# Segment decays of a Mamba-2 scan in a hybrid decoder layer: from products of TensorE to running sums spread by DMA

## What is computed

```python
a_cum = jnp.cumsum(adt, axis=-1)
decay = jnp.exp(segsum(adt))                 # exp(cs[l] - cs[s]) for s <= l, else 0
cb = jnp.einsum("bclhn,bcshn->bhcls", cc, bc)
y_diag = jnp.einsum("bhcls,bcshp->bclhp", cb * decay, xc)
to_end = jnp.exp(a_cum[..., -1:] - a_cum)
states = jnp.einsum("bclhn,bclhp->bchpn", bc * to_end[..., None], xc)
# scan over chunks: h -> chunk_decay * h + states, from h0 = 0
y_off = jnp.einsum("bclhn,bchpn->bclhp", cc * from_start[..., None], prev)
y = (y_diag + y_off) + d_skip * x            # then gate with SiLU(z), RMSNorm in 2 groups
```

## Time and profile before

| | before |
|---|---|
| median of 3 runs | 1161.25 us (1160.11 to 1161.86) |
| profiled execution, its own time | 1160.93 us |
| its span | 1159.0 us |
| TensorE busy | 1096.3 us, 95% |
| VectorE busy | 872.1 us, 75% |
| ScalarE busy | 548.6 us, 47% |
| GpSimd busy | 242.4 us, 21% |
| mean granted clock of TensorE | 0.975 |

### The profile page before, as it was taken

One profiled execution on the slowest core, in us unless ns is written; L12 is line 12 of the kernel. 1 busy time (PEld: TensorE's weight loads), 2 busy tenths in 40 slices (PEclk: granted clock), 3 DMA queues, 4 the chain that ended last, 5 costly groups with the idle time before them and its releaser, 6 DMA issues.

```text
span 1159.0 us, 14934 instructions
## 1 busy us (share of the span) xinstructions
PE 1096.3 (95%) x5144; PEld 876.8 (76%) x5144; DVE 872.1 (75%) x1137; ACT 548.6 (47%) x964; POOL 242.4 (21%) x235
## 2 busy tenths in 40 slices
PE   2699999999999999969999999999999999999997
PEld 2578767666777777747888888888888888888885
DVE  5769577767559566587888888888888886776687
ACT  3631255555553343565454444454445455454453
POOL 2100011121212333124333333333333100000012
PEclk7699999999999999989999999999999999999999
DMA  9988311001132101104344343434353496733224
GB/s 342 328 252 300 111 37 37 19 20 37 37 110 91 55 37 55 55 37 146 119 153 139 133 152 119 158 129 158 109 170 109 143 370 220 237 100 98 93 91 164
DMA packets 115359, 152.71 MB, mean 132 GB/s; under 512 B 15148, under 2 KB 75117, under 8 KB 115309
## 3 DMA queue, kind: packets, MB, share of 16 engines
q1 hardware_dynamic: 114989, 151.00, 38.9%
q0 software_dynamic: 320, 1.06, 0.3%
HBM read 121.10 MB, written 30.95 MB: 131 GB/s over the span
## 4 chain that ended last, share of the span: by engine, by line
PE 85%; DVE 6%; ACT 3%; DMA 2%; issue 1%; POOL 1%; SPq 1%; DVEq 0%; POOLq 0%; ACTq 0%
PE ps L2283 34%; PE ps L1938 24%; PE ps L2348 17%; PE ps L1977 2%; PE ps L2003 1%; PE ps L1991 1%; PE ps L2127 1%; DVE big L1255 1%; DMA raw<-in_w_in_dram 1%; ACT big L973 1%; DMA scratch<-in_rel_bias_dram 1%; PE ps L2219 1%; PE ps L2042 1%; DVE a_lo L1524 0%; DVE scratch L1462 0%
## 5 line engine op out<-in xcount | busy, mean ns | idle before, releaser
L1938 PE MATMUL ps<-a_hi,w_hi 128*128 128x512 f32 x416 | 146.1, 429 | 9.0 <-DVE a_lo L1315 6.2
L1938 PE MATMUL ps<-a_lo,w_hi 128*128 128x512 f32 x416 | 132.3, 396 | 0.0
L1938 PE MATMUL ps<-a_hi,w_lo 128*128 128x512 f32 x416 | 131.6, 395 | 0.0
L2348 PE MATMUL ps<-w_hi,a_hi 128*128 128x512 f32 x308 | 119.9, 389 | 0.2 <-DVE a_lo L1771 0.2
L2348 PE MATMUL ps<-w_hi,a_lo 128*128 128x512 f32 x308 | 119.8, 389 | 0.0
L2348 PE MATMUL ps<-w_lo,a_hi 128*128 128x512 f32 x308 | 119.8, 389 | 0.0
L1938 PEld LDWEIGHTS ps<-a_hi,w_hi 128*128 128x128 f32 x416 | 73.6, 192 | 32.6 <-issue 21.9
L1167 ACT ACTIVATE w_hi<-raw 128x512 fp32r<-128x512 f32 x77 | 48.8, 634 | 98.2 <-PE ps L2348 88.4
L1087 ACT ACTIVATE scratch<-ps 128x512 f32<-128x512 f32 x88 | 52.3, 595 | 88.8 <-PE ps L2283 88.7
L1938 PEld LDWEIGHTS ps<-a_hi,w_lo 128*128 128x128 f32 x416 | 78.9, 190 | 18.3
L1938 PEld LDWEIGHTS ps<-a_lo,w_hi 128*128 128x128 f32 x416 | 78.9, 190 | 18.2 <-issue 0.5
(11 more groups left out here) (246 smaller groups left out, 2431.5 us busy)
## 6 DMA issues: line engine op xcount, KB each, us to landing
big<-in_w_ada_dram SPq DMA_DIRECT2D x24, 1024.0 KB, 9.0
raw<-in_w_up_dram SPq DMA_DIRECT2D x22, 512.0 KB, 5.0
big<-in_w_up_dram SPq DMA_DIRECT2D x22, 512.0 KB, 4.6
big<-in_w_down_dram SPq DMA_DIRECT2D x22, 512.0 KB, 6.4
down_weight_sums<-big SPq DMA_DIRECT2D x22, 512.0 KB, 3.4
raw<-down_weight_sums SPq DMA_DIRECT2D x44, 256.0 KB, 2.8
ffn_hidden<-big SPq DMA_DIRECT2D x21, 512.0 KB, 2.6
big<-ffn_hidden SPq DMA_DIRECT2D x21, 512.0 KB, 7.9
```

What stands on the lines that cost most here:

```text
L1938: mm = pe.matmul(out, lhs_of[a], rhs_of(b, j), start=first and p == 0, stop=last and p == 2)
L2348: mm = pe.matmul(bk, a[:, ts], rhs_op(s)[w], start=fresh and m == 0, stop=last and m == 2, skip_group_check=s // KH in (J6, J3, J7))
```

## The change

The decays exp(cs[l] - cs[s]) are no longer made from sums on TensorE for each chunk.
- `dt_sum` makes one more product, the running sums of all chunks with heads on partitions (`sum_rows`, 64 rows of 128), and VectorE also takes the negated sums as columns (`neg_sums`). SP stores the rows to DRAM (`rows_d`) and, for each chunk, `load_decay(i)` reads the chunk's 4 KB row into all 128 partitions of `decay`, once y_diag of the chunk before has read it.
- GpSimd adds a mask of -1e30 where s > l (`decay_mask`, in place of `decay_terms`). ScalarE makes eight exponentials of 128x128 a chunk, each with a column of `neg_sums` as bias.
- `ssd_weights` multiplies by the CB products straight from bank 7. `cbm` and its product by `upper` are gone, with the two products against `strict`.
- Chunk 0 has no y_off and no decay of the state, since the state is zero; the last chunk makes no B rows, no state product and no state. GpSimd's memset of the state is gone.
- The lists are put in another order: on TensorE state_product(i) stands right behind y_diag(i), z_transpose(0) goes into the last input unit, and projection 0 ahead of y_off(1). On VectorE the attention half of the low parts goes from behind mixed_norm to ahead of ssm_rows of the block before. On ScalarE the attention half of the high parts and the exponentials of chunk i+1 go ahead of gated_squares(i).
- The semaphores of the token sums (t1 to t4) are merged into one.

The core of the diff:

```diff
+            def load_decay(i):
+
+                if i >= 1:
+                    sp.wait_ge(s_yd, i)
+                sp.dma_start(scratch[:, 2048:3072], rows_d[i:i + 1, :].to_broadcast([P, H * P])).then_inc(s_kl, 16)
...
+                if k == 0:
+                    sp.wait_ge(s_kr, 1)
+                    sp.dma_start(rows_d.rearrange("b (h l) -> (b h) l", h=H), sum_rows).then_inc(s_ks, 16)
+                    sp.wait_ge(s_ks, 16)
+                    load_decay(0)
...
+                if k == 6:
+                    load_decay(1)
             sp.wait_ge(s_wlo, U_OUT + 4)
             load_xr(0)
             load_xr(1)
+            load_decay(2)
...
             for b in range(NB):
+                if b + 3 < NB:
+                    load_decay(b + 3)
                 sp.wait_ge(s_mx, b + 1)
...
-            def decay_terms(i):
-
-                if i >= 1:
-                    pool.wait_ge(s_yd, i)
+            def decay_mask(i):
+
+                pool.wait_ge(s_kl, 16 * (i + 1))
                 for g in range(GROUPS):
-                    adt = dtv[:, ADT, i * H + 4 * g:i * H + 4 * g + 4].unsqueeze(2).to_broadcast([P, 4, P])
-                    tri = upper.unsqueeze(1).to_broadcast([P, 4, P])
-                    pool.tensor_tensor(decay[:, g, :].rearrange("p (h l) -> p h l", h=4), tri, adt,
-                                       ALU.mult).then_inc(s_rd, 1)
+                    dg = decay[:, g, :].rearrange("p (h l) -> p h l", h=4)
+                    pool.tensor_tensor(dg, dg, no_future.unsqueeze(1).to_broadcast([P, 4, P]),
+                                       ALU.add).then_inc(s_rd, 1)
...
             def decay_exp(i, g):
-                act.wait_ge(s_D, 2 * i + g + 1)
-                act.activation(decay[:, g, :], bank(5 + 2 * g), ACT.Exp).then_inc(s_E, 1)
+
+                act.wait_ge(s_rd, 2 * i + g + 1)
+                for h in range(4):
+                    part = decay[:, g, h * P:(h + 1) * P]
+                    n = i * H + 4 * g + h
+                    ins = act.activation(part, part, ACT.Exp, bias=neg_sums[:, n:n + 1])
+                ins.then_inc(s_E, 1)
...
+            for i in range(2, NB + 1):
+                if i < NB - 1:
+                    b_rows(i)
+                if i < NB:
                     mixed_squares(i - 2)
+                mixed_hi_ssm(i - 1)
...
+                x1_squares(i - 2)
                 if i < NB:
+                    mixed_hi_attention(i)
+                    if i + 1 < NB:
+                        for g in range(GROUPS):
+                            decay_exp(i + 1, g)
+                    gated_squares(i)
                     x1_evacuate(i - 2)
...
             w_out_lo(0)
+            y_diag(0)
+            gate_y(0)
+            state_step(0)
             w_out_lo(1)
+            w_out_lo(2)
+            mixed_lo_attention(0)
+            ssm_rows(0)
+            w_out_lo(3)
             ssd_rows(1)
+            w_out_lo(4)
+            mixed_lo_ssm(0)
...
-                if i >= 1:
-                    pe.wait_ge(s_g, i)
-                pe.wait_ge(s_rd, 2 * i + 1)
-                pe.matmul(bank(5), strict, decay[:, 0, :], start=True, stop=True).then_inc(s_D, 1)
-
-            def second_sums(i):
-                pe.wait_ge(s_cbm, i + 1)
-                pe.wait_ge(s_rd, 2 * i + 2)
-                pe.matmul(bank(7), strict, decay[:, 1, :], start=True, stop=True).then_inc(s_D, 1)
...
                     y_off_product(i)
                     y_diag_products(i)
+                    if i < NB - 1:
+                        state_product(i)
                 project_out(i - 1, range(0, 2))
-                if i < NB:
-                    state_product(i)
                 project_out(i - 1, range(2, 4))
```

More of the change, by code:

```diff
@@ L717, in _ @@
                 normalise_probs(u)
-                if u == 28:
-                    pool.wait_ge(s_dte, 1)
-                    decay_terms(0)
-            pool.wait_ge(s_si, len(SILU) - 2)
-            link(pool.memset(state, 0.0))
+                if u == 30:
+                    pool.wait_ge(s_nf, 1)
+                    decay_mask(0)
             def weight_sums(p, par, first=False):
@@ L756, in _ @@
                     rstd(st[:, 58:60], st[:, 56:58], SSM_W // GROUPS, s_gr)
+                if i < 2:
+                    decay_mask(i + 1)
                 if i == 3:
@@ L1661, in _ @@
                     mixed_norm(i - 2)
-                mixed_lo(i - 1)
+                mixed_lo_ssm(i - 1)
                 if i == NB:
@@ L1673, in _ @@
                     y_diag(i)
-                    state_step(i)
+                    if i < NB - 1:
+                        state_step(i)
                     gate_y(i)
@@ L1677, in _ @@
                 if i < NB:
+                    mixed_lo_attention(i)
                     ssm_rows(i)
@@ L2052, in rows_and_b @@
                     pe.wait_ge(s_bn, i)
-                for g in range(GROUPS):
-                    mm = pe.transpose(bank(4)[:, g * P:(g + 1) * P], blk(BB + g, i), ident)
-                mm.then_inc(s_bT, 1)
+                if i < NB - 1:
+                    for g in range(GROUPS):
+                        mm = pe.transpose(bank(4)[:, g * P:(g + 1) * P], blk(BB + g, i), ident)
+                    mm.then_inc(s_bT, 1)
                 if i == 0:
```

212 lines of the change are left out of this document (110 added, 102 removed).

## The result

The changed kernel takes 1152.64 us in the median of 4 runs (1151.6 to 1154.91), the kernel before 1161.55 beside it (median, 1160.11 to 1162.09). The ratio is 0.9928, with a 95% interval of 0.991 to 0.9946: faster by 0.72%, or 8.4 us (the two medians differ by 8.9). The forecast was 1150.0, range 1146 to 1159.

A forecast was written before the change was run, and what follows sets the result against it. TensorE, busy 95% of the span, was taken as the bound. Terms 12.2 + 1.1 - 1.2 - 0.9 = 11.2 us took the profiled 1160.93 to 1149.7; against the median 1161.25 the forecast was 1150.0, range 1146 to 1159.

The forecast's parts named there:

- One block: Out-projection stage: period 17.83 us instead of 20.28, a gain of 2.45 counted five times, 12.2 us.
- Weight sums: One block where GpSimd's weight sums slow ssm_rows, 2.90 instead of 0.88 us, with little slack: -0.9 us.
- Last block: Chunk 7 makes no B transposes and no state product: a gain of 1.1 us.
- The loop of decays: Decay load to y_diag: load landing time L plus 12.5 us, L taken as 4.0, fitting the period up to 5.3.
- rival C: Blocks: DMA becomes the bound, L above 7.8; at 8.2 period 20.7, 1167 us; chance 0.10 slower, 0.04 within the bound.
- B: Rival: decays land late, L 6 to 6.8, period 18.5 to 19.3, time 1154 to 1158.7 us; chance 0.12.
- what would show it: Expected trace signs, among them 17.8 us periods, loads landing in about 4 us, mask waiting for the x1 root, not DMA.
- The opening: Chunk 0 up to projection 1: 0.5 us gained at the same clock, 1.7 lost to a lower clock, in all -1.2.
- The clock: Opening: TensorE's granted clock falls after the idle wait before projection 0, as at the token sums; 1.7 us lost.
- dt_sum, the term put at nothing: dt_sum: a new 128-column product of 0.22 us and two small copies, beside units where TensorE hardly waits.
- Rival A: Opening: the clock holds and w_out_lo(4) meets nothing; 2.3 us better, 1147.7 us; chance 0.12.
- D: Rival for the blocks: the sums were never on the path, the low-half wait sets the block; excluded as a whole.

The follow-up runs named there:

- the first profile: Profile of the changed kernel with nothing further edited, taken in its first group of runs; that execution took 1154.91 us, the slowest of four (median 1152.64).
- the product in the gap: Changed kernel plus one unused 128x512 product for chunks 2 to 7 between two projections, ahead of the mixed transposes: 1152.82 us, ratio 0.9932.
- the second profile: Profile from running the changed kernel again as it is, with nothing edited: median 1152.38 us over 5 runs, ratio 0.9925.
- the reordered opening: Changed kernel with VectorE's order in the opening rewritten and the masks of chunks 1 and 2 held behind the normalised rows: 1147.56 us, ratio 0.9884.
- the filled kernel: Changed kernel plus unused products in TensorE's two waits ahead of projection 0, five before mixed_transpose(0) and four behind: 1151.2 us, ratio 0.9908.

## Why the prediction was right, and where it was not

The forecast of 1150.0 was 2.6 us too low, its sign and its range held. In the terms of its sum the first profile has 12.4 for the blocks (12.2 - 0.9 in the forecast), 1.0 for the last (1.1), -2.9 for the opening (-1.2) and -0.6 ahead of the mark (nothing): 9.9 us against 11.2. The second has 185.85 - 175.99 - 0.6 = 9.3. The runs say 8.4 to 8.9; the last 0.4 to 1.5 us have no place here, and two profiles of the same kernel differ by more than that behind x1_transpose(7) (644.3 and 642.9) and up to the mark (4 us). Point by point:

- **One block.** Forecast 17.83, measured 17.42 to 17.71 in the four undisturbed ones; over the five blocks the gain is 12.4 us, where I had 12.2 less 0.9 for the weight sums. The two parts of the block shown above: from the projection's start to the mixed transposes 13.65 (forecast 13.5), from there to the next projection 4.07 (forecast 4.35). The second is the mis-sized one. I had taken the chain of before with its 0.38 us of "issue" at the end; here that is 0.11. That this chain still sets the gap, by 0.34, the product in the gap shows. The gain of 0.6 from the attention halves is shown twice, undone (+0.62) and made alone (-0.54).
- **Weight sums.** Forecast -0.9. ssm_rows of that block took 2.93 us beside them, like the 2.90 of the earlier trace rows, and the period was 18.58 where its neighbours were 17.44 and 17.42: -1.1. Right, and by the cause named:

```profile
408.00 2.93 DVE L1669 SCALAR_TENSOR_TENSOR big<-big,st,normw 128x256 f32<-128x256 f32 x2 [1.38 <-POOL st L704]
```

- **Last block.** Forecast 1.1, measured 1.0.
- **The loop of decays.** Forecast L + 12.5 with L = 4.0 and a limit of 5.3. The loads landed in 3.7 us in the median:

```profile
DMA to landing us min/median/max: 3.3/3.7/5.5
...
420.13 2.96 POOL L728 TENSOR_TENSOR scratch<-scratch 128x512 f32<-128x512 f32 x2 [0.34 <-DMA scratch<-decay_sums_by_row]
421.88 2.53 ACT L1011 ACTIVATE scratch<-scratch 128x128 f32<-128x128 f32 x8 [2.79 <-POOL scratch L728]
```

  The exponentials took 2.5 us and not 2.9, the rest of the loop 12.1. The load made twice shows the loop where it binds, on the slower side of the kernel before, which is rival C at L = 8.4. The choice of the nearest row, the x blocks of the same size, was right for most of the loads, and C did not occur. B did, in one block of the second profile, where the loads took 3.5 to 6.4 us, 4.0 in the median. The slowest was that of chunk 3:

```profile
373.75 1.97 PE L2174 MATMUL ps<-big,scratch 128*128 128x64 f32 x16 [1.23 <-DVE scratch L1505]
375.75 0.34 SPq L529 DMA_DIRECT2D scratch<-decay_sums_by_row  x1
...
382.19 2.98 POOL L728 TENSOR_TENSOR scratch<-scratch 128x512 f32<-128x512 f32 x2 [2.89 <-DMA scratch<-decay_sums_by_row]
...
392.40 1.97 PE L2174 MATMUL ps<-big,scratch 128*128 128x64 f32 x16 [0.70 <-DVE scratch L1505]
```

  From the end of y_diag (375.72) to the mask it is 6.5 us, and with 12.1 for the rest the loop gives 18.6; the period was 18.65, where the first profile has 17.44 with a load of 4.6. So the margin that I called enough was used up once, at a cost of 1.2 us. SP issues the store of a residual 1.15 us behind that load; whether it slows the load was not tested. In the block of the first profile shown above the mask waited 0.34 us for the DMA, not for the root: the root had been done for 0.3 us. That sign in "what would show it" was wrong in kind and harmless in size.
  The estimate of 5.1 us from the Trainium skill ("DMA: Bandwidth & Descriptors", Anatomy of one DMA and Bandwidth) is above the medians of 3.7 and 4.0 and below the slowest loads, 5.5 and 6.4. The page gives its figures there for DMAs that GpSimd issues; these are SP's.
- **The opening, the term that failed.** Forecast -1.2, measured -2.9. Projection 0 was to start 2.1 us before the old one, and came 0.3 before it. The step that was mis-sized is "gate to ssm_rows is some 5 us": from the end of the z transposes (345.42) to the end of ssm_rows(0) (352.58) it is 7.2. Behind it the queue ran as added up, 4.7 us to the end of `mixed_lo_ssm(0)` (357.25). I had placed the collision of the mask at w_out_lo(4), with 0.6 us, and taken ssm_rows(0) at 0.9. The mask came straight behind the root on GpSimd, and with it stood ssm_rows(0), the step that the same root releases. It took 2.88. The root itself was slowed by w_out_lo on VectorE: 0.75 and 1.58 us, where the same two instructions took 0.22 and 0.72 in the reordered opening, with next to nothing beside them.
  The Trainium skill's rule that I quoted ("SBUF - State Buffer", Who interferes with whom) says this: two such instructions exclude each other, each time one whole instruction. The trace agrees by its 2.88. I had applied the rule to the blocks, where there was slack, and to one place of the opening, but not to the step on the path. Taking the mask away from there gave 1.4 us of time, with intervals that overlap, and not 2.0; VectorE's ssd_rows and the clock stood next in line. Together with VectorE's order it gave 4.8.
- **The clock.** Forecast 1.7 us lost after an idle wait. It was 0.84, 0.50 and 0.60 in the three stretches of the opening, and the first two tiles took 4.56 us against the 2.80 of the filled kernel: 1.76. From projection 0 to projection 1 I had 23.2 us with this loss and the trace has 23.1. Right in size. But filling the wait did not bring the 1.7 us back for good: the low clock came at the next wait, 20 us later.
- **dt_sum, the term put at nothing.** I had its new product at 0.22 us, "beside units in which TensorE hardly waits". It took 0.36 (297.65 to 298.01), and because TensorE hardly waits there, it all counts: 0.6 us with what is around it.

By the chances: the forecast's own range, 1148.5 to 1153, held the time, and luck had a part in it: the blocks gave 1.1 us more than the sum, the opening 1.7 less. Rival A did not occur, D fell with the products put back: one in the projection costs its full length.

## To carry to other kernels

When work moves from TensorE to GpSimd, don't look at GpSimd's share but at the instruction that its predecessor releases on VectorE: if both start from the same event, they can meet every time, and the one on the path pays for it (here 2.0 us, where ssm_rows took 2.88 instead of 0.88). Add up both sides of a gap, the engine's own work and the chain that it waits for; the longer one sets the gap, and only the difference between them is free. A loop through DRAM is safe up to the L at which it equals the period, and is best measured by making L longer. Judge it by the slowest load and not by the median: at 4.0 us in the median, one load of 6.4 took the block over the limit.

## What the runs showed of the hardware

- A row of 4 KB in DRAM spread to 128 partitions (512 KB) lands in 3.3 to 5.5 us, 3.7 in the median, in the first profile and in 3.5 to 6.4, 4.0 in the median, in the second. That is near a plain block of 512 KB (3.4 in the earlier trace rows) and mostly not like the broadcasts in the crowd of the start (6.8, 8.2). Reading the same 4 KB for every partition cost at most 0.3 to 0.6 us in the median.
- Eight exponentials of 128 columns with a bias, SBUF to SBUF, took 2.43 to 2.53 us, where eight activations of the same size from PSUM took 2.9.
- TensorE at the lower granted clock is not tied to long waits only: y_diag took 3.17 us behind a wait of 1.89 in one kernel and 1.97 us behind a wait of 1.55, with the clock falling right after it, in another. In the changed kernel the clock was at 0.50 from 351 to 361.2 us and at 1.00 behind the wait of 1.22 us ahead of y_diag(2); with TensorE's two waits filled it was at 1.00 there and fell behind a wait of 1.19 us at 374.7 (one profile).
- A step of 0.68 us on VectorE takes 1.8 beside a mask of GpSimd whose instruction takes 1.3 to 1.7, and GpSimd's own small steps grow from 0.22 and 0.72 to 0.75 and 1.58 beside a long step of VectorE. The exclusion works both ways.
